# Winograd pairs for the gate projections: GpSimd makes the second operand's remainder ahead of the two sums over spent raw weights, in both blocks

## The reference, cut to what matters

```python
# first block
p = h @ w_in[i]
... ga, gb = jnp.split(p, offsets, axis=-1)[-2:]
out_b = short_conv_branch(cb, cc, cx, conv_w[i])
merged = (jax.nn.sigmoid(ga + bg_a) * (out_a @ w_proj_a[i])
          + jax.nn.sigmoid(gb + bg_b) * (out_b @ w_proj_b[i]))
# second block
gates = jax.nn.sigmoid(proj[..., B_Z1:G1] + b_gate)
merged = gates[..., :D_MODEL] * y_a + gates[..., D_MODEL:] * y_b
```

## Time and profile before

| | |
|---|---|
| runs | 2902.57 us median of 3 (2895.04 to 2903.45) |
| profiled execution | 2906.81 us, of which the span of its instructions is 2905.0 us |
| granted clock of PE, mean over the span | 0.991 |
| PE busy | 2795.2 us, 96% |
| POOL busy | 1361.0 us, 47% |
| ACT busy | 1131.7 us, 39% |
| DVE busy | 1592.1 us, 55% |

### The profile page before, as it was taken

How to read it: one execution, slowest core, us unless ns; L and a number is a source line. 1 busy time by engine, 2 the same in 40 slices (tenths; PEclk the granted TensorE clock), 3 DMA queues, 4 the chain that set the end, 5 groups by cost and what they waited for, 6 DMA issues and landing times. The chain is left out here.

```text
span 2905.0 us, 48675 instructions
## 1 busy us (share of the span) xinstructions
PE 2795.2 (96%) x19923; PEld 2243.7 (77%) x19923; DVE 1592.1 (55%) x1910; ACT 1131.7 (39%) x1819; POOL 1361.0 (47%) x1022
## 2 busy tenths in 40 slices
PE   8999788999999999999999999999999899999999
PEld 6767677778888877788888888678777678866787
DVE  7354444863465444555555554777768435357651
ACT  6333233554311134424444443433323335567410
POOL 2431214677645443347777775211221457645551
PEclk9999899999999999999999999999999999999999
DMA  6243333343171111213222223032335534422243
GB/s 230 88 169 124 96 92 100 109 136 89 37 231 44 54 48 44 67 57 101 89 90 91 88 95 109 15 107 60 88 94 130 165 92 128 122 92 66 85 129 124
DMA packets 318495, 288.93 MB, mean 99 GB/s; under 512 B 47844, under 2 KB 270235, under 8 KB 315596
## 3 DMA queue, kind: packets, MB, share of 16 engines
q1 hardware_dynamic: 318110, 285.91, 32.4%
q10 hardware_dynamic: 174, 0.04, 0.0%
HBM read 214.86 MB, written 70.65 MB: 98 GB/s over the span
## 5 line engine op out<-in xcount | busy, mean ns | idle before, releaser
L179 POOL TENSOR_TENSOR w_lo<-w_raw,w_hi 128x1024 fp32r<-128x1024 f32 x87 | 226.9, 2609 | 358.5 <-ACT w_hi L174 354.4
L282 PE MATMUL ps<-h_hi,w_hi 128*128 128x512 f32 x960 | 309.7, 404 | 3.1 <-PEq L6512 1.6
L857 POOL TENSOR_TENSOR op_lo<-w_raw,op_hi 128x512 fp32r<-128x512 f32 x172 | 222.5, 1301 | 184.8 <-ACT op_hi L846 184.3
L282 PE MATMUL ps<-h_lo,w_hi 128*128 128x512 f32 x960 | 297.4, 391 | 0.0
L282 PE MATMUL ps<-h_hi,w_lo 128*128 128x512 f32 x960 | 296.2, 390 | 0.0
L161 POOL TENSOR_TENSOR w_hi<-w_raw,ones 128x1024 fp32r<-128x1024 f32 x54 | 132.7, 2457 | 278.7 <-PE ps L282 204.0
L282 PEld LDWEIGHTS ps<-h_hi,w_hi 128*128 128x128 f32 x960 | 178.6, 188 | 59.7 <-issue 24.8
L282 PEld LDWEIGHTS ps<-h_hi,w_lo 128*128 128x128 f32 x960 | 180.7, 188 | 38.7
L282 PEld LDWEIGHTS ps<-h_lo,w_hi 128*128 128x128 f32 x960 | 180.8, 188 | 38.5
L1786 DVE TENSOR_TENSOR x_t<-x_t,ps 128x512 f32<-128x512 f32 x144 | 96.2, 685 | 83.6 <-PE ps L912 56.8
L846 ACT CAST op_hi<-w_raw 128x512 fp32r<-128x512 f32 x167 | 102.5, 620 | 88.1 <-POOL w_raw L862 27.4
(11 more groups left out here) (757 smaller groups left out, 7289.3 us busy)
## 6 DMA issues: line engine op xcount, KB each, us to landing
w_raw<-in_w_in_dram SPq DMA_DIRECT2D x91, 512.0 KB, 4.8
mix_gates<-mix_sig SPq DMA_DIRECT2D x64, 256.0 KB, 2.3
w_raw<-in_w_up_dram SPq DMA_DIRECT2D x32, 512.0 KB, 4.2
w_raw<-in_w_down_dram SPq DMA_DIRECT2D x32, 512.0 KB, 3.4
kv_raw<-in_w_kv_dram SPq DMA_DIRECT2D x16, 512.0 KB, 6.2
mix_gate_b<-mix_gates SPq DMA_DIRECT2D x32, 256.0 KB, 5.4
mlp_t3h<-mlp_kept_t SPq DMA_DIRECT2D x6, 1024.0 KB, 5.0
mlp_t3l<-mlp_kept_t SPq DMA_DIRECT2D x6, 1024.0 KB, 5.0
```

The lines of the kernel that those rows point to most:

```text
L179: eng.tensor_tensor(c.w_lo[:, s], c.w_raw[:, s], c.w_hi[:, s].bitcast(F32), ALU.subtract).then_inc(c.w_split, 1)
L282: last = pe.matmul(o, w[:, s, k], a[:, k - offset, (half + h) * width:(half + h + 1) * width], start=(k == kts[0] and w is c.w_hi and a is ...
L857: pool.tensor_tensor(self.lo(o)[:], src, self.hi(o)[:].bitcast(F32), ALU.subtract).then_inc(self.pooled, 1)
```

## The change

In `pool_products` the remainder of operand 1 (`self.rest(pool, o + 1)`) moves from behind the two sums s3 and s2 to ahead of them. The counts at which the others wait follow, in a table of `PairStream`'s own: product 1 waits for 3 operations of the pair in place of 5, the rounding of s3 (m=4) for 4 in place of 3, that of s2 (m=2) for 5 in place of 4. No operation is added or removed, and all 18 pairs of both blocks follow it.

```diff
@@ class PairStream(MlpStream):
+    SUM1, LO0, LO1, SUM4, SUM2, LO2, LO3, LO4, SUM5, LO5, LO6 = range(1, 12)
+    FIRST = PairOrder((2, 3, 6, 7, 8, 10, 11), {1: 1, 2: 5, 4: 4, 5: 9}, {0: (0, 0), 2: (0, 0), 3: (0, 1), 4: (1, 0), 6: (1, 1)}, (9, 11))
+
@@ def pool_products
         self.sum_into(pool, self.sum(o + 1), a21, a22, ALU.add, 0)
         self.wait_loaded(pool, unit)
         self.rest(pool, o)
+        self.rest(pool, o + 1)
         self.sum_into(pool, s3, a21, a11, ALU.subtract, count + self.SUM1)
         self.sum_into(pool, s2, s3, a22, ALU.add, count + self.SUM4)
         first_sums()
-        self.rest(pool, o + 1)
         before_third()
         for m in (2, 3, 4):
             self.rest(pool, o + m)
```

## The result

The changed kernel takes 2907.68 us (median of 20 runs, 2904.24 to 2912.92), the kernel before 2901.91 us in the same measurement (20 runs, 2895.04 to 2906.84). The ratio is 1.0020 with an interval of [1.0014, 1.0026]: 0.2% slower, 4 to 7.5 us. The forecast was 2901.7 us in a range of 2894 to 2907; the time lies above that range.

What follows compares the result with a forecast made beforehand. PE was taken to bound the kernel, busy 96% of the span. A gain of 0.9 us in the first block's pair 1, nothing elsewhere, gave 2902.57 - 0.9 = 2901.7 us, range 2894 to 2907.

Steps and rivals of the forecast that it cites:

- What bounds the kernel, and the place in the first block: PE bounds, busy 96% of the span; only the first block's pair 1 matters, where 3.66 us is all to gain.
- The remainder of m=1 goes ahead: First block's pair 1: PE no longer waits, product 1 starts 1.99 us earlier at full clock; gain so far 3.66 us.
- The sums go back: First block's pair 1: sums end 1.68 us later, seed_u comes last, PE pauses 2.1 us before product 2; gain 1.5 us.
- The side job behind it: First block's pair 1: later branch_hi and branch_lo put L2934 at 576.5 to 577.5, leaving a gain of 0.4 to 1.5 us.
- the gain of 0.9 us: First block's pair 1: the middle of the 0.4 to 1.5 us left after the side job, taken off the median 2902.57.
- the 1.67 us of slow clock: First block's pair 1: time PE loses in product 1 because the granted clock is 0.51; counted as gained.
- the fall at the new pause: Rival, first block's pair 1: the clock falls before product 2, which loses 1.67 us; time 2902.7 us, chance 0.35.
- The 17 other pairs cost nothing as long as product 2's remainder keeps its slack: All other pairs: s2 ends 1.30 to 1.74 us later, but product 2 has at least 3.3 us to spare; no cost.
- the slack is not there: Rival: later rounding holds up product 2; 17 pairs cost 44 us, 2946 us, or 2912 with part of them; chance 0.04.
- 0.3% is what a measurement can tell: Whole kernel: earlier runs reach from 2895.04 to 2903.45, so about 0.3% (8.7 us) can be told from no change.

Runs made afterwards that it cites:

- its repetition: The changed kernel, new order in all 18 pairs, measured once more for a second profile: 2910.48 us against 2905.22 of the kernel before, ratio 1.0010.
- the first block alone: Against the kernel before, the new order in the first block's 12 pairs only, the second block in the old order: 2904.06 us against 2903.42, ratio 1.0002.
- the square moved: The changed kernel with the second block's side-job square on ACT ahead of the rounding for m=2: 2904.32 us against 2903.42 of the kernel before, ratio 0.9999.
- the second block alone: Against the kernel before, the new order in the second block's six pairs only: 2909.02 us against 2903.42, ratio 1.0016.
- its pair 1 alone: Against the kernel before, the new order in pair 1 of the second block only: 2908.01 us against 2903.42, ratio 1.0008.
- its pairs 2 to 5 alone: Against the kernel before, the new order in pairs 2 to 5 of the second block only: one run, 2902.73 us.
- the late square: The kernel before, old order everywhere, with the second block's side-job square on ACT behind `seed_u` instead of ahead: 2919.9 us against 2904.23, ratio 1.0048.
- `seed_u` moved: Against the kernel before, the first block's pair 1 alone in the new order, its `seed_u` ahead of the rounding for m=2: 2904.63 us against 2904.23, ratio 0.9998.

## Why the prediction was wrong

**What bounds the kernel, and the place in the first block:** right as far as it goes: PE waited for a moved remainder nowhere else. That a list of PE's waits is also the size of what can be lost was not right; see the failed step.

**"The remainder of m=1 goes ahead", "The sums go back":** right, and close. The wait for the remainder is gone, `seed_u` comes last before product 2, and the pause is 2.06 us where 2.1 was worked out.

**"The side job behind it":** too large. It was to take back up to 1.1 us by holding L2934; in both profiles of the changed kernel L2934 follows product 2 without a wait.

**The clock in the first block:** the gain of 0.9 us was a gain by the clock. The forecast took the 1.67 us of slow clock as gained and the fall at the new pause as a rival with a chance of 0.35. In four profiles of the new order (after, its repetition, the first block alone, the square moved) the clock fell three times; in five of the old order in that pair (before, the second block alone, its pair 1 alone, its pairs 2 to 5 alone, the late square) four times. With the fall the pair takes 12.38 to 12.43 us in the old and 12.52 to 12.53 in the new order, without it 10.83 and 10.94. A slow old pair set against a fast new one (12.38 and 10.94) gives the upper end of the forecast's 0.4 to 1.5 us; at equal clock the new order gains nothing there.

**"The 17 other pairs cost nothing as long as product 2's remainder keeps its slack":** this is the step that failed, in two ways. The slack was read at the wrong consumer. Product 2 had its 3 to 5 us, and no pair lost time there. But the held rounding also holds what is queued behind it on ACT, and the list was followed only to `seed_u` and, in the first block, to the side job. In the second block the square stands between (the description of ACT's list ahead of the prediction leaves it out), and is wanted one product earlier: 0.56 us of slack. And the delay was too small: "one remainder, 1.30 to 1.74 us" supposed that the rounding for m=1 is done when POOL comes to it. That holds in the first block's pair 1, where ACT is idle; in the second block's pair 1 POOL waits 1.72 us for it, which the sums had covered, so that s2 came 3.0 us late. No list of waits could show this: before the change PE never waited at line 3006 in the pairs, and a consumer with 0.56 us to spare looks there like one with 5. The experiments with the square moved either way show the cause: with it ahead the loss is gone, with it behind PE waits for it, and loses time, without the change. How the 3.0 us of delay come about is read from the rows; no run took the wait for the rounding away by itself.

**The rivals:** "the slack is not there" named the right kind of mechanism, with 10 us "with part of the pairs", and gave it 0.04. That was the case, at 4.7 us, through another instruction than the one it watched. The statement that 0.3% is what a measurement can tell was too wide as well: with 20 runs of each kernel the interval is +-0.06%.

**What is left open:** how much of the measured 5.8 us is scatter. The two stages explain 4.7 us in two profiles; the interval begins at 4 us, so nothing more is needed, and nothing more was shown. The scatter goes with the clock: of the 20 runs of the changed kernel, the seven with a mean granted clock of 0.989 took 2907.59 to 2912.92 us, the four with 0.992 took 2904.24 to 2905.89. In which stage the clock fell in runs without a profile isn't known, so how often the change costs 3.0, 4.7 or 6.3 us in the second block stays open.

## What to carry to other kernels

When a wait on an in-order engine comes later, follow every instruction queued behind it, in each stage that shares the code, to the engine that wants it next, and compare the delay with the smallest slack found; here the operand that was watched had 3.3 us to spare, the one that lost the time 0.56. A list of waits shows who is late, not who is nearly late. A filler between two dependent operations (here two sums between a rounding and its remainder) may be what hides the other engine's latency: when it is moved away, ask in each place whether the result is there. When an engine is late for its data, look at what the fetch is queued behind before reordering the work: the fetch moved ahead of one load was worth 3 us here, the reordering less than nothing. And when a gain at one place is worked out, compare both versions at the same granted clock.

## What the runs showed of the hardware that was not expected

PE pauses of only 1.2 us were followed by a fall of the granted clock in four of five cases (the late square), and the fall cost about 1.6 us each time in PE's pace. Behind the pause of 1.17 us in the first block (`seed_u` moved) it stayed up. At the same pause of 1.8 us in the second block's pair 1 the clock fell in two of four profiles (after and its repetition; not in the second block alone nor in its pair 1 alone), for 1.6 us of cost in one and 3.2 in the other. The Trainium skill (TensorE: Matmul & The Clock Gate, "Part 1: The HAM clock gate") has the window in which activity is looked at run free of the kernel; a fall that comes and goes at the same place agrees with that.
